# Prompt attention of a streaming encoder layer: scores computed already turned, in split fp32r, with the row maximum as an extra contraction row

## The reference, cut to what matters

```python
q, k = _rmsnorm(q, q_norm_g), _rmsnorm(k, k_norm_g)      # per head of 64
lf = jax.nn.log_sigmoid(f_logit + b_f)
c_all = jnp.cumsum(jnp.concatenate([lf_hist, lf], axis=1), axis=1)
...
s = jnp.einsum('bqhd,bkhd->bhqk', q_blk, k) * scale
s = s + cq_blk[..., None] - ckT
s = jnp.where(k_pos[None, :] <= q_pos[:, None], s, NEG_INF)
p = jax.nn.softmax(s, axis=-1)
return jnp.einsum('bhqk,bkhd->bqhd', p, v)
```

## Time and profile before

| | |
|---|---|
| median of 3 runs | 2732.37 us (2718.83 to 2754.99) |
| profiled execution, time | 2734.04 us |
| profiled execution, span | 2732.4 us |
| mean granted TensorE clock | 0.918 |
| busy in the span: PE / DVE / ACT / POOL | 85% / 49% / 37% / 6% |
| `attend` | from about 100 to 1125 us |

### The profile page before, as it was taken

The page is one execution under the profiler, slowest core; times in us unless marked ns, Lnnn a source line. Parts: engine busy times, 40 slices in busy tenths (PEclk is TensorE's granted clock), DMA queues, the critical chain, the costliest instruction groups (busy, mean ns, idle before and its releaser), DMA issues. The chain is left out here.

```text
span 2732.4 us, 37076 instructions
## 1 busy us (share of the span) xinstructions
PE 2316.4 (85%) x12096; PEld 1849.0 (68%) x12096; DVE 1336.0 (49%) x1639; ACT 1020.5 (37%) x1315; POOL 169.6 (6%) x175
## 2 busy tenths in 40 slices
PE   4678979898997989799899949989908999999991
PEld 2666858676776866699878849975505766666660
DVE  5345453545455453311255542212136888788874
ACT  3133222323323222211156632101106777777760
POOL 0111010101001000000011100000020000000002
PEclk9789999899989996799999979999958999999995
DMA  3210211302020110211245542133037999999986
GB/s 93 61 40 18 63 32 47 79 0 79 0 79 14 42 53 3 97 46 46 82 151 184 160 142 66 38 138 107 0 131 272 386 372 370 373 365 377 372 313 226
DMA packets 206037, 376.83 MB, mean 138 GB/s; under 512 B 19377, under 2 KB 127193, under 8 KB 205945
## 3 DMA queue, kind: packets, MB, share of 16 engines
q1 hardware_dynamic: 184776, 302.27, 32.7%
q0 software_dynamic: 17600, 61.18, 7.0%
q10 hardware_dynamic: 3584, 12.58, 1.2%
HBM read 301.60 MB, written 74.39 MB: 138 GB/s over the span
## 5 line engine op out<-in xcount | busy, mean ns | idle before, releaser
L1854 DVE TENSOR_TENSOR e_w_lo<-e_raw,e_w_hi 128x2048 fp32r<-128x2048 f32 x192 | 437.6, 2290 | 113.4 <-ACT e_w_hi L1781 101.0
L1781 ACT CAST e_w_hi<-e_raw 128x2048 fp32r<-128x2048 f32 x192 | 366.7, 1912 | 132.9 <-DMA e_raw<-w_down_e 53.5
L1154 ACT ACTIVATE probs_s<-scores,neg_max 128x256 f32<-128x256 f32 (+7 forms) x128 | 95.0, 742 | 446.4 <-DVEq L84 446.0
L1254 DVE COPY probsT<-turn_ps 128x512 f32<-128x512 f32 (+4 forms) x232 | 131.5, 567 | 249.1 <-PE turn_ps L1024 225.7
L101 PE MATMUL proj_ps<-w_qkv_hi,xh 128*128 128x384 f32 x544 | 194.5, 358 | 9.3 <-PEq L285 9.3
L1044 PEld LDWEIGHTS out_ps<-v_new,probsT 128*128 128x128 f32 x1152 | 160.1, 210 | 60.8 <-DVEq L84 44.3
L1044 PE MATMUL out_ps<-v_new,probsT 128*128 128x64 f32 x1152 | 180.6, 298 | 20.2 <-DVEq L84 19.0
L103 PE MATMUL proj_ps<-w_qkv_hi,xl 128*128 128x384 f32 x544 | 184.8, 340 | 0.0
L102 PE MATMUL proj_ps<-w_qkv_lo,xh 128*128 128x384 f32 x544 | 184.6, 339 | 0.0
L1240 DVE TENSOR_REDUCE neg_max<-scores 128x1 f32<-128x256 f32 (+7 forms) x128 | 97.0, 758 | 150.5 <-PE scores L1002 120.0
L1000 PE MATMUL scores<-qkT 65*128 65x512 f32 (+3 forms) x384 | 160.6, 532 | 5.8 <-DVEq L84 4.9
(11 more groups left out here) (363 smaller groups left out, 4967.1 us busy)
## 6 DMA issues: line engine op xcount, KB each, us to landing
e_raw<-w_gate_e SPq DMA_DIRECT2D x64, 1024.0 KB, 13.8
e_raw<-w_up_e SPq DMA_DIRECT2D x64, 1024.0 KB, 14.1
e_raw<-w_down_e SPq DMA_DIRECT2D x64, 1024.0 KB, 13.0
slot_x<-zrows POOLq DMA_DIRECT2D x48, 440.0 KB, 6.3
e_x<-slot_x SPq DMA_DIRECT2D x33, 384.0 KB, 11.1
w_qkv<-w_in SPq DMA_DIRECT2D x24, 512.0 KB, 10.0
slot_y<-e_y ACTq DMA_DIRECT2D x32, 384.0 KB, 6.2
slot_y<-zrows POOLq DMA_DIRECT2D x24, 352.0 KB, 9.6
```

Of the source, the lines that this page charges most:

```text
L1154: chain(sc.activation(probs[n % 2][:, 0:w], half(n)[:, 0:w], ACT.Exp, bias=neg_max[:, n:n + 1], accum_out=total[:, n:n + 1]), exp_ready)
L1254: chain(v.tensor_copy(probsT[q % 2][0:rows, 0:len(js) * P], turn_ps[0:rows, m % 2, 0:len(js) * P]), turn_taken[m % 2])
L1781: sc.copy(w_hi[u][:, :], w.raw[c][:, :]).then_inc(wh_ready, 1)
L1854: v.tensor_tensor(w_lo[u][:, :], w.raw[c][:, :], w_hi[u][:, :], ALU.subtract).then_inc(wl_ready, 1)
```

## The change

For a pair, a unit is now one head and 512 queries (four units); a step is one unit and one tile of 128 keys (24 steps of 128 to 512 queries). The scores are computed turned, keys on the partitions, so that exp's output is directly the operand of the product with v, and the 72 transposes of probabilities and their copies are gone.

- q and k are split in high and low fp32r parts. `high` holds the high parts and three more rows: for keys -c (high part), -c (low part) and ones, for queries ones, ones and minus the maximum. `cross` holds 128 rows, the high part of q against the low part of k and the other way round. `score(s)` is one product with 67 rows, one with 128, and the mask.
- The maximum of each query row must be known before. `max_chunk(n)`, PE: 24 pieces of up to 512 keys, one fp32r product of the high parts (66 rows), all into the one bank `max_ps`; `maximum`, DVE: takes each. `turn_rows`, PE: 16 small fp32 products a pair bring four maxima columns to a row in three copies' place; ACT copies them into `high`. PE waits for `max_taken` before each piece.
- `exp(s)`, ACT: no bias, no sum. `weigh(s)`, PE: one fp32 product a step, stationary `v_one` (64 columns of v beside 64 columns of ones, per head), moving the probabilities, up to 512. The output is turned already and its other 64 rows hold the row sum; `take_out(u)`, DVE: a reciprocal of 64x512 and a product 64x512, four times a pair.
- `take_qk` (ACT) and `take_cross` (DVE) replace the copy to `qkT`: five batches of two tiles, 18 transposes; ACT makes four casts and DVE four differences per batch, POOL copies `high` into `cross` twice. Past keys of both heads are turned together, 16 transposes. The weights are loaded, rounded and split in thirds. The maxima of the first unit of the next pair, and its rows, are in the edge (`EDGE`).

```diff
+    UNITS = [(0, 0), (0, 1), (1, 0), (1, 1)]
+    STEPS = [(u, j) for u in range(4) for j in range(4 * (UNITS[u][1] + 1))]
+    MAXES = [(u, t, c0) for u in range(4) for t in range(4 * UNITS[u][1], 4 * UNITS[u][1] + 4) for c0 in range(0, (t + 1) * P, BANK)]
...
+    MAX_AT = {0: (4, 5, 6, 7), 1: (8, 9, 10, 11), 5: (12,), 6: (13,), 7: (14,), 8: (15,),
+              9: (16, 17), 10: (18, 19), 11: (20, 21), 12: (22, 23)}
+    ROWS_AT = {2: 1, 9: 2, 13: 3}
+    PAST_AT = {18: 0, 19: 1, 20: 2, 21: 3}
+    W_AT = {18: (0, 1), 22: (2,)}
+    ROOT_AT, NORM_AT = 19, {20: 0, 21: 1, 22: 2}
...
+    EDGE = (("qk", 0), ("qk", 1), ("p", 0), ("max", 0), ("qk", 2), ("weigh", 0), ("max", 1), ("p", 1), ("qk", 3),
+            ("weigh", 1), ("max", 2), ("p", 2), ("weigh", 2), ("max", 3), ("qk", 4), ("p", 3), ("rows", 0), ("weigh", 3),
+            ("p", 4), ("weigh", 4))
...
+        max_ps = scores[:, 0:BANK]
+        st_ps = [scores[:, (1 + b) * BANK:(2 + b) * BANK] for b in range(2)]
+        out_ps = [scores[:, 3 * BANK:4 * BANK], out_b[:, :]]
...
+                    last = te.matmul(max_ps[:, 0:w], high[0:HD + 2, h, 0, t * P:(t + 1) * P], high[0:HD + 2, h, 1, c0:c0 + w],
+                                     start=True, stop=not diagonal)
...
+                        if s >= 2:
+                            pe.wait_ge(exp_ready, i * NS + s - 1)
...
+                        te.matmul(out[:, 0:q1 - q0], high[0:HD + 3, h, 1, j * P:(j + 1) * P], high[0:HD + 3, h, 0, q0:q1],
+                                  start=True, stop=False)
+                        last = te.matmul(out[:, 0:q1 - q0], cross[:, h, 1, j * P:(j + 1) * P], cross[:, h, 0, q0:q1],
+                                         start=False, stop=not diagonal)
...
+                        te.matmul(out_ps[u % 2][:, q0 - c * BANK:BANK], v_one[:, j, h, :], probsT[s % 2][:, 0:q1 - q0],
+                                  start=(j == 0), stop=(s == last_step(u)), skip_group_check=True).then_inc(pv_done, 1)
...
+                                pe.wait_ge(max_taken, i * NM + n)
+                                alone(pe, g)
+                                max_chunk(n)
...
-                    def turn_group(q):
-                        n, js = owner[q]
...
+                        sc.activation(probsT[s % 2][:, 0:q1 - q0], st_ps[s % 2][:, 0:q1 - q0], ACT.Exp).then_inc(exp_ready, 1)
...
+                    for b in range(BATCHES):
+                        m = use["qk", b]
+                        act.wait_ge(turned, turned_count(i, m))
+                        alone(act, g)
+                        take_qk(b, m % 2)
+                        if b == 1:
+                            soft_stream()
+                    rows(0, i + 1)
...
+                        chain(v.reciprocal(recip[mine, :], out_ps[u % 2][other, :]))
+                        chain(v.tensor_tensor(out_T[mine, c * BANK:(c + 1) * BANK], out_ps[u % 2][mine, :], recip[mine, :], ALU.mult), out_taken)
```

820 lines of the change are left out of this document (498 added, 322 removed).

## The result

The changed kernel takes 2855.5 us (median of 4 runs, 2837.0 to 2865.3) against 2738.7 us for the kernel before on the same chip: ratio 1.042, 95% interval 1.033 to 1.051. It is slower, where 2708 us was forecast, and lies outside the range of 2630 to 2790. Each ratio in this document is taken against runs of the kernel before on the same chip. It leaves out executions in a slower state (e1, e10 and e12 have some), which the printed median holds.

What follows compares the result with a forecast made beforehand. PE was taken as the bound. From 2734 us profiled, seven pairs give -23, the last pair -11, the head +5: 2705, lengthened for unseen waits to 2708 us (-1.0%); 8 in 10 range 2630 to 2790.

Steps and rivals of the forecast that it cites:

- the terms of the maxima's waits and of half clock: Steps 0 to 17: maximum waits of 6.6, 1.4 and 0.5 us, half clock 2 us at a pair's start.
- if the clock does in the steps what it does now only in the last pair: Sign of being wrong: PE's clock in a pair's steps falls to half, as it mostly did in the last pair.
- maximum pieces that start 1.3 us apart in steps 9 to 12: Sign of being right: the single bank's round trip, put at 1.34 us, shows between piece starts.
- Steps 18 to 23: End of a pair, without projection: ACT's list is the bound, 13.7 us against 8.3 us of PE work.
- it ends at 13.8 and PE's stream products wait for it: Edge: DVE's take_out(3), with a 3.35 us reciprocal, ends 13.8 us after the stream's scores start; whole edge 30.1 us.
- Half clock in the edge: Slower rival: PE is granted 0.5 from step 18 to the next pair; pair 132, total 2806 us; chance 0.13.
- The rival by which waits stay at 25.9 us: Faster rival: a pair's losses remain 25.9 us beside 83.7 of work; pair 109.6, total 2627 us; chance 0.27.
- The rival by which fewer transposes keep the clock up: Faster rival: last pair at full clock, 105.9 to about 65, pairs lose 2 us; total 2661 us; chance 0.05.
- The price of fp32 for fp32r products: Slower rival: fp32r products cost what fp32 costs, +35 us a pair, near 2990 us; chance 0.02.
- The last pair: Pair without projections: 82 us at the old ratio of time to work plus about 13 of maximum waits: 95, -11.
- five batches at 1.9, four maximum pieces and rows about 14 us instead of 8: Ahead of the first pair: part of the head's +5 us, which was put between -3 and +12.
- up to 2.2 us for each third of the split: Shared SBUF reads: each third of POOL's weight split can hold a DVE norm that long; 0 to 4 us a pair.

Runs made afterwards that it cites:

- e1: The changed kernel with the maximum taken over the diagonal block of 128 keys alone, 16 pieces instead of 24: 2739.5 us, ratio 1.000.
- e10: e9 with idle PE products that change no result, 20 in steps 19 to 23 and 28 in the edge: 2553.8 us, ratio 0.935.
- e12: e2 with all maximum pieces and their masks back on PE, but nothing reads or waits for them: 2707.5 us, ratio 0.988.
- e2: The changed kernel without any maximum; the query's own cumulative gate, loaded by DMA, is the softmax offset: 2642.0 us, ratio 0.969.
- e4: The changed kernel with the reciprocal of the sums replaced by a copy, so prompt outputs are not the reference's: 2837.3 us, ratio 1.036.
- e5: The changed kernel with its maximum pieces spread out, no work added or removed: 2771.0 us, ratio 1.015.
- e7: e2 with another order in the edge: probabilities transposed through the prompt's score banks, last sums taken out earlier, DVE order of its own: 2591.9 us, ratio 0.947.
- e3: The changed kernel with idle PE products that change no result, in steps 18 to 23 and the edge: 2833.6 us, ratio 1.035.
- e9: e7 plus alternating projection banks, early load of exp's table, and two thirds of the next pair's weights rounded and split earlier: 2575.0 us, ratio 0.946.

## Why the prediction was wrong

**Steps 0 to 17: the terms of the maxima's waits and of half clock were mis-sized.** The prediction had 62.9 of work and 12 of waits, 75 together; 84.0 came. The work was nearly right: the pieces take 5.0 by e12 against 4.3 counted, 0.7 more. Without any maximum e2 takes 62.3 us against 56.0 of work, 1.5 of waits for ACT and 2 of half clock, 59.5: 2.8 more, of which its 5.1 us at half clock explain 0.5 and the rest is open. The maxima's term is the larger miss. The prediction put 6.6 + 1.4 + 0.5 = 8.5 us on maxima and rows beyond their work, and e12 leaves 16.7 - 2.6 = 14, 5.6 more. A round trip is 1.52 us, not 1.34, which makes 1.1 in six places. The rest has the size of the clock: half clock was put at 2 us "at the start of a pair, as now", but the changed kernel stands at half for 13.7 us of these steps where e2 does for 5.1, and half of that difference is 4.3 (an estimate; in e4 one such stretch cost 1.55). So "if the clock does in the steps what it does now only in the last pair", one of the prediction's own signs of being wrong, came true in part. The maxima and their places have a part in this, since it shrinks without them (e2) and with their spreading (e5, 3.4 us at half); how much of the 14 us is wait and how much clock, no run parts cleanly. The mechanism of the waits was named, and its row predicted ("maximum pieces that start 1.3 us apart in steps 9 to 12": they do, at 1.52). That it could be avoided by an order alone, 10 us a pair, wasn't seen.

**Steps 18 to 23** were right (13.7 against 14.2, ACT's list).

**The edge: the step "it ends at 13.8 and PE's stream products wait for it" failed.** They start at 720.55, 20.8 us behind the stream's first score. Of the 7.0 us, 3.4 are the scores at half clock, which was the rival's price. Another 1.9 are hand-overs: `take_out(3)` ends 19.05 us behind the first score, 5.25 later than forecast, since between PE, ACT and DVE each one takes 0.3 to 0.4 us in these rows. The last 1.7 the sum left out: behind `take_out(3)` DVE still has to copy the probabilities (0.69, end 719.86) with a hand-over on either side. Behind that point 16.3 was forecast and 20.0 came; of those 3.7 the first product group at half clock (2.05 instead of about 1.1) is one, the rest isn't parted. The reciprocal had exactly its estimated 3.35 us, and e4 prices it at 2.6 in the edge. What the prediction took as given is the order: e7 needs 9 to 10 us less for more or less the same instructions.

**The rivals.** Half clock in the edge was given 0.13 and 2806 us. The clock was indeed 0.50 in the edge, but from 698.0 to 725.3 and not from step 18 to the next pair. Its mechanism is worth 4 us a pair by e3, less than a third of its price of 13.2 (132 against 118.8); that PE is not the engine that others wait for in most of the edge would explain this, but wasn't tested alone. That the result came out even beyond this rival is due to steps 0 to 17 and to the order of the edge. The rival by which waits stay at 25.9 us was the opposite of what happened: at 139.8 against 83.7 of work there are 56. The rival by which fewer transposes keep the clock up forecast a last pair at full clock and about 65 us: with fewer transposes alone its clock went from 0.61 to 0.69 and its time to 91.2. It is 0.80 and 61.8 us in e2, where the maxima go too. The price of fp32 for fp32r products didn't come: the second score product takes 0.24 us for 512 columns (740.84 to 741.08).

**The last pair** was right in size (91.2 against 95) and wrong in its parts, so that this is luck. The prediction had 82 for everything but maximum waits, and 13 for these. e12, which has the pieces but not their waits or the rows, takes 65.9, and the waits and rows are 25.3: two errors of 12 to 16 us that cancel. The 82 carried over the ratio of time to work of the last pair before, which ran at a clock of 0.61; e12's runs at 0.83, and part of the 25.3 is again the clock (0.69 in the changed kernel).

**The head: the term "five batches at 1.9, four maximum pieces and rows about 14 us instead of 8" was mis-sized.** The +5 became 16 us. PE's first transpose of q and k and the first score, in the kernel before and in the changed one:

```profile
155.09 7.34 PE L949 MATMUL turn_ps<-ident,qk_sb 128*64 128x128 f32 x36 [14.81 <-DVEq L84]
...
163.28 0.48 PE L1000 MATMUL scores<-qkT 65*128 65x128 f32 x2 [0.84 <-ACTq L84]
```
```profile
153.43 1.97 PE L1013 MATMUL turn_ps<-ident,qk_sb 128*128 128x128 f32 x8 [10.13 <-DVEq L84]
...
175.23 0.76 PE L1084 MATMUL scores<-qk_high 67*128 67x512 f32 x1 [1.34 <-ACT qk_high L1290]
```

Up to the first transpose the prediction was right: the first projection ends 3.0 us later (forecast 5), and from there the way is 4.7 us shorter (forecast 6), since POOL's split no longer holds a norm (7.3 us for one of 0.96 before). But from the first transpose to the first score 21.8 us pass instead of 8.2, 13.6 more where 6 were forecast, all at half clock. Without the first unit's maxima and rows e2 needs 11.4, so these are 10.4 of it. The remaining 4.2 come behind the first score. There the split, which has moved behind all transposes (166.41 instead of 145.53), does hold up the first maximum piece and with it the projection, but shows only 1.56 us of wait; and e9, which moves it away again, gains 2.0 us at the first store.

**The shared reads.** By the Trainium skill ("SBUF — State Buffer", "Who interferes with whom") a DVE operation with two SBUF inputs contends with a GpSimd one that reads SBUF, and from it the prediction estimated up to 2.2 us for each third of the split. The trace agrees in kind: a pair's first norm, which starts while the split runs, takes 1.35 us and the next ones 0.96, 0.4 us a pair. In e9 one norm takes 3.01 us, nearly the whole estimate: what it costs depends on where the two meet.

Together: seven pairs of +21.0, +11 in the head and -4 in the last pair give 154. With the forecast's 2705, before its margin of 3, that is 2859, and 6 more lie behind the last store, where nothing was changed (1614.0 us instead of 1607.8): 2865, as measured for the profiled execution.

## What to carry to other kernels

A value that one engine must fetch from another through a single buffer costs its whole round trip wherever two uses stand together. Read it from start to start and not from the idle column, and look for longer work to stand between before counting instructions saved. Count the clock as well: a change can add microseconds at half clock in a dense stretch, which no idle column shows (13.7 us a pair here, 3.4 with the pieces spread). Ask whether the value is needed at all: an offset in softmax that is known beforehand serves when the exponent is bounded, here by normalised q and k and a gate difference that is never above zero. When work is moved, price it at its new place; and where four engines pass work round in a short stretch, write out each one's list: the order of the edge alone was worth 8.4 us a pair here (113.1 to 104.7), nearly as much as the whole change once it had no maximum (122.15 to 113.1).
